# Six parameter loads issued by ScalarE's queue instead of SP's at the start of a hybrid S5 / RG-LRU / PEER step

## The chip, the cores and the metric

One core of a Trainium2 chip runs the whole kernel; the other cores are idle. The metric is the device time of one execution in microseconds. The kernel before takes 3084.43 us, the median of three runs (3083.14 to 3085.8). Its engines are TensorE (PE), VectorE (DVE), ScalarE (ACT), GpSimd (POOL) and SyncE (SP), each with its own instruction stream, and 16 DMA engines that serve transfers issued by any of them.

## The reference, cut to what matters

One layer over 1024 prompt tokens and 8 decode tokens, all in float32, width 1024:

```python
def layer(x, ...):
    h = rmsnorm(x, norm_mix)
    proj = h @ w_in                       # 1024 x 3584
    u_s5, x_lru, y_lru, g_a, g_b = jnp.split(proj, SPLITS, axis=-1)
    a_out, s5_re, s5_im = s5_branch(u_s5, h0_re, h0_im, lam_re, lam_im, log_dt, ...)
    b_out, lru_h, new_buf = rglru_branch(x_lru, y_lru, conv_buf, lru_h0, ...)
    merged = (jax.nn.sigmoid(g_a) * (a_out @ w_proj_a)
              + jax.nn.sigmoid(g_b) * (b_out @ w_proj_b))
    x = x + merged @ w_out
    x = x + peer(rmsnorm(x, norm_ffn), w_q, sub_keys, u_tab, v_tab)   # 8 heads x 16 experts a token
    return x, (s5_re, s5_im, lru_h, new_buf)
```

The parameters that matter here are small: `log_dt` (one value per S5 group), `lam_re` and `lam_im` (the S5 eigenvalues), `norm_mix` (the gain of the first norm), and a packed table of biases and convolution weights. The S5 branch needs `exp(lam * exp(log_dt))` before it can scan; the first projection needs `x * norm_mix`.

## The kernel before, in words

The prompt is worked in chunks of 256 tokens (four of them, the last with the 8 decode tokens beside it). A chunk runs the norm, the projections, the S5 and RG-LRU branches, the mixing, the PEER queries and the choice of experts; then its 256 gather slots (one indirect transfer each, 128 rows of 8 KB) are used by DVE (dot products) and PE (weighted sums), interleaved with the dense work of the next chunk. The first chunk's dense work has no gathers beside it.

What matters here is the first 20 us. Each engine's stream is written out by hand.

SP (from line 620) first issues the two halves of the first chunk's columns of x, 512 KB each, as 128 rows of 4 KB (line 622). Then come the six small parameter loads (lines 645 to 648): two halves of `log_dt`, each one 64-byte row broadcast to 64 partitions, then `lam_re`, `lam_im`, `prm` and `nmix`, each 128 short rows. All six count on one semaphore, `step_in`. Then the loop over `load_weights(0, l)` issues the first two pairs of weight blocks of `w_in`, 1024 KB each as 128 rows of 8 KB (line 634). Then eight more parameter loads (line 653) and one for the block-diagonal gate weights (line 654). Later weight loads wait until PE has freed a slot of the ring (`slot_free`).

ACT's stream starts at line 1176: a dummy square root of one column, which makes the first table load happen early; then the squares of the two halves of x (`norm_squares`), each as soon as its half has landed; then it waits for `step_in`, and makes eight blocks of `raw`, that is x times `nmix`, at 0.41 us a block; then the square root of the norm (`norm_root`). All its activations have line 807 in the profile.

DVE's stream starts at line 1253 with two memsets, then waits for `step_in` (all six loads) before anything else: the exponential of `log_dt` by a polynomial, `norm_mean` (which needs PE's sum of squares), more small parameter work, the reciprocal of the norm (line 1246), and `first_units(0)` (line 1212), which needs PE's first projected unit.

PE's stream: warm-up matmuls on ones (line 2457 on), the sum of squares (`norm_sum`, line 2012), and then the units of the first projection (line 2037). A unit's matmul t waits for block t of `raw` and, at its start, for its weights.

Of the kernel before, what the change touches and what calls it, by code (L numbers as in the profile page):

```python
# [356 lines left out]
def build(nc, i_, o_):  # L357

    with ExitStack() as ctx:
# [6 lines left out]
        def sem(name):  # L366
            return ctx.enter_context(nc.semaphore(name))
# [47 lines left out]
        nmix = T.take(KT)  # L415
        nffnT, nfinT = T.take(KT), T.take(KT)
        prm = T.take(40)
# [20 lines left out]
        lre, lim, ldt, th = (S.take(SJ) for _ in range(4))  # L438
# [73 lines left out]
        step_in = sem("step_in")  # L512
# [83 lines left out]
        def flat(v):  # L596
            return v.rearrange("p a b -> p (a b)")
# [21 lines left out]
        def _(sp):  # L619
# [22 lines left out]
                    before = c if at >= 0 else c - 1  # L642
                    sp.wait_ge(unit, units(before) + slot_unit(before, PAIRS[before][at][-1]) + 1)

            for g2 in range(2):
                sp.dma_start(ldt[64 * g2:64 * g2 + 64, :], i_["log_dt"][g2].partition_broadcast(64)).then_inc(step_in, 16)
            for name, dst in (("lam_re", lre), ("lam_im", lim), ("prm", prm), ("nmix", nmix)):
                sp.dma_start(dst, i_[name]).then_inc(step_in, 16)
            for l in range(2 * RING):
                load_weights(0, l)  # L650
            for name, dst in (("b_raw", braw), ("c_raw", craw), ("s5_0", s0), ("sconv", sconv), ("slru", slru),
# [153 lines left out]
        def _(act):  # L805
# [215 lines left out]
            def chunk(c, last):  # L1021
# [149 lines left out]
                if last:  # L1171

                    act.wait_ge(s8_out, 16 * HEADS)
                    act.dma_start(flat(sS[0:NS * HEADS, 0:2]), s8_dram.rearrange("t h k -> (t h) k")).then_inc(s8_in, 16)

            act.sem_inc(sum_ok, 1)
            act.wait_ge(const_ok, 1)
            af(rt2, ones[:, 0:1], ACT.Sqrt)
# [1372 lines left out]
```

## Time and profile before

| | |
|---|---|
| median of three runs | 3084.43 us (3083.14 to 3085.8) |
| span of the profiled execution | 3084.7 us |
| PE busy, matmuls | 2367.6 us, 77% |
| DVE busy | 2150.7 us, 70% |
| POOL busy | 1202.5 us, 39% |
| ACT busy | 1001.2 us, 32% |
| DMA | 1226.32 MB, mean 398 GB/s |
| DMA queue of POOL (q0) | 148608 packets, 1082.20 MB |
| DMA queue of SP (q1) | 27440 packets, 136.67 MB |
| DMA queue of ACT (q10) | 1648 packets, 4.85 MB |

The page gives no time for the profiled execution other than its span, 3084.7 us, which lies 0.3 us above the median and inside the three runs. Busy time is the time in which an engine worked; the chain of waits is the path of work and releases that ended last, followed back from the end. The shares are of the whole span, and the change touches less than its first hundredth, so the page as a whole says little; the rows below are of the stretches that count.

### The profile page before, as it was taken

The page shows a single profiled execution, that of the slowest core. Times are in us where ns is not written, and L with a number is a line of the kernel's source. Part 1 is how long each engine was busy: PE and PEld are TensorE (multiplying, and loading weights), DVE is VectorE, ACT ScalarE, POOL GpSimd, SP SyncE. Part 2 cuts the span into 40 slices and gives each one's busy share as a digit, 9 for nine tenths or more (in the row PEclk, how much of TensorE's full clock was granted, in tenths as well). Part 3 has the DMA queues.
Part 4 walks back from the last instruction along what each step waited for, and adds up shares of the span by engine and source line. Part 5 has one row for each costly group of instructions (what it writes and reads, how often), then busy time and mean ns, then how long its engine had stood idle before and what let it go on. Part 6 is the DMA issues. An engine that isn't in the chain of part 4 may idle for free.

```text
span 3084.7 us, 40759 instructions
## 1 busy us (share of the span) xinstructions
PE 2367.6 (77%) x14560; PEld 1190.1 (39%) x14560; DVE 2150.7 (70%) x5361; ACT 1001.2 (32%) x3275; POOL 1202.5 (39%) x1048
## 2 busy tenths in 40 slices
PE   9997769888876778789777678888987676555565
PEld 7864325555343334455233324444433331111111
DVE  7758887765579887665468887766558897544445
ACT  2224332422334332432234332432233443222223
POOL 0013343443344443343343443434344444444442
PEclk9999889999999989989988879999998886777777
DMA  4569999999999999999999999999999999999997
GB/s 154 208 244 398 420 421 420 415 414 399 420 420 418 420 420 419 418 392 420 420 419 417 421 420 408 420 394 420 418 420 420 420 416 419 416 406 420 420 419 328
DMA packets 177898, 1226.32 MB, mean 398 GB/s; under 512 B 22664, under 2 KB 23048, under 8 KB 32160
## 3 DMA queue, kind: packets, MB, share of 16 engines
q0 software_dynamic: 148608, 1082.20, 84.9%
q1 hardware_dynamic: 27440, 136.67, 11.2%
q10 hardware_dynamic: 1648, 4.85, 0.4%
q8 instruction: 115, 1.88, 0.3%
q14 instruction: 87, 0.71, 0.1%
HBM read 1219.09 MB, written 4.55 MB: 397 GB/s over the span
## 4 chain that ended last, share of the span: by engine, by line
DMA 45%; PE 26%; DVE 15%; ACT 5%; POOL 3%; issue 3%; ACTq 1%; DVEq 0%; SPq 0%; POOLq 0%
DMA arena<-in_uv,arena 44%; PE psum L2140 11%; DVE arena L1718 7%; PE psum L2037 7%; ACT arena L807 4%; POOL arena L759 3%; PE psum L2184 3%; DVE arena L1212 3%; PE psum L2204 2%; DVE arena L1220 1%; DMA arena<-in_w_ab 1%; PE psum L2216 1%; ACT L807 1%; ACTq L831 1%; DVE arena L1590 1%
## 5 line engine op out<-in xcount | busy, mean ns | idle before, releaser
L759 POOL DMA_INDIRECT arena<-in_uv,arena x1032 | 1199.3, 1162 | 1856.2 <-PE psum L2140 1525.3
L1718 DVE CUSTOM_DVE_ANT_0 arena<-arena 128x1024 f32<-128x1024 f32 x1024 | 1246.8, 1225 | 789.4 <-DMA arena<-in_uv,arena 781.5
L2140 PE MATMUL psum<-arena 64*64 64x512 f32 x8184 | 1226.7, 723 | 669.9 <-ACT arena L807 622.5
L807 ACT ACTIVATE arena<-arena 128x1 f32<-128x1 f32 (+4 forms) x2746 | 727.1, 302 | 1850.8 <-DVE arena L1718 1741.9
L2140 PEld LDWEIGHTS psum<-arena 64*64 64x64 f32 x8184 | 301.2, 151 | 1401.1 <-ACT arena L807 923.5
L2037 PE MATMUL psum<-arena 128*128 128x256 f32 (+1 forms) x2656 | 632.4, 393 | 7.7 <-ACT arena L807 6.9
L2037 PEld LDWEIGHTS psum<-arena 128*128 128x128 f32 x2656 | 504.3, 194 | 193.6 <-issue 121.8
L1212 DVE TENSOR_TENSOR arena<-arena 128x256 f32<-128x256 f32 (+12 forms) x561 | 249.9, 472 | 12.1 <-issue 0.4
L807 ACT ACT_TABLE_LOAD x119 | 152.7, 1283 | 11.2 <-DVE arena L1212 7.1
L807 ACT ACTIVATE arena<-psum 128x256 f32<-128x256 f32 (+5 forms) x254 | 98.3, 402 | 144.9 <-PE psum L2037 94.4
L2184 PE MATMUL psum<-arena 128*128 128x128 f32 (+2 forms) x640 | 123.6, 351 | 9.5 <-DMA arena<-in_w_ab 7.2
L2184 PEld LDWEIGHTS psum<-arena 128*128 128x128 f32 x640 | 103.2, 196 | 37.2 <-issue 19.4
L1220 DVE SCALAR_TENSOR_TENSOR arena<-arena 128x256 f32<-128x256 f32 (+8 forms) x287 | 99.0, 357 | 19.3 <-ACT arena L807 13.9
L2204 PE MATMUL psum<-arena 128*128 128x512 f32 x192 | 90.3, 614 | 0.0
L1718 DVE DVE_READ_ACCUMULATOR2_ANT arena<- 128x1 f32 x1024 | 83.6, 82 | 0.0
L1486 DVE TENSOR_TENSOR_SCAN arena<-arena 128x64 f32<-128x64 f32 x256 | 68.9, 331 | 1.3
L1220 DVE SCALAR_TENSOR_TENSOR arena<-arena,psum 128x128 f32<-128x128 f32 (+4 forms) x97 | 46.0, 513 | 33.6 <-PE psum L2184 28.9
L2216 PE MATMUL psum<-arena 128*128 128x256 f32 (+1 forms) x320 | 63.2, 354 | 0.4 <-issue 0.4
L1212 DVE TENSOR_TENSOR arena<-psum,arena 128x512 f32<-128x512 f32 (+2 forms) x91 | 59.6, 684 | 2.8 <-PE psum L2140 1.8
L2216 PEld LDWEIGHTS psum<-arena 128*128 128x128 f32 x320 | 52.6, 200 | 22.5 <-issue 17.8
L2204 PEld LDWEIGHTS psum<-arena 128*128 128x128 f32 x192 | 35.2, 193 | 56.3 <-issue 56.3
L2052 PEld LDWEIGHTS psum<-arena 32*128 32x128 f32 x512 | 35.0, 207 | 28.9 <-issue 26.2
(134 smaller groups left out, 981.9 us busy)
## 6 DMA issues: line engine op xcount, KB each, us to landing
arena<-in_w_in SPq DMA_DIRECT2D x56, 1024.0 KB, 9.0
arena<-in_w_q SPq DMA_DIRECT2D x34, 1024.0 KB, 9.4
arena<-in_uv,arena POOLq DMA_INDIRECT x1032, 13.7
arena<-in_w_ab SPq DMA_DIRECT2D x12, 1024.0 KB, 9.4
arena<-in_w_out SPq DMA_DIRECT2D x11, 512.0 KB, 15.8
arena<-in_keys SPq DMA_DIRECT2D x17, 256.0 KB, 8.3
arena<-in_w_ab SPq DMA_DIRECT2D x8, 512.0 KB, 10.8
arena<-in_x_tok SPq DMA_DIRECT2D x8, 512.0 KB
```

What stands on the lines that cost most here:

```text
L759: pool.indirect_dma_start(uvring[:, r], None, i_["uv"], bass.IndirectOffsetOnAxis(column, 0)).then_inc(uv_in[r], 16)
L807: return nc.scalar.activation(out, in_, f, **kw)
L1212: return V.tensor_tensor(out, a, b, op)
L1220: return V.scalar_tensor_tensor(out=out, in0=a, scalar=s1, in1=b, op0=op0, op1=op1)
L1486: return V.tensor_tensor_scan(v, mag2[:, j:j + 1].to_broadcast([P, SEG]), v, start, ALU.mult, ALU.add)
L1718: V.tensor_tensor_reduce(out=u, in0=u, in1=hn[i // (SLOT // 2)], scale=1.0, scalar=0.0, op0=ALU.mult, op1=ALU.add, accum_out=dots_[:, b % ...
L2037: ins = mm(PB[u % 2][:, 0:n], w[:, P * t:P * t + P], rhs[:, t, 0:n], start=(t == 0), stop=(t == k - 1))
L2052: ins = mm(SB[j % 2][:, 2 * SEG * part:2 * SEG * part + 2 * SEG], wT[o:o + 32, QT * (2 * r + part) + q], uS[o:o + 32, q, 2 * SEG * r:2 * S ...
L2140: ins = mm(PV[o:o + HP, half], dg[r:r + HP, PAIR * (b % 2) + k], uvring[r:r + HP, place(c, i) % UV, at:at + 512], start=(i % (SLOT // 2) = ...
L2184: ins = mm(banks[side][:, 0:cols.stop - cols.start], w[:, 512 * side + P * t:512 * side + P * t + P], src[:, t, cols], start=(t == 0), sto ...
L2204: ins = mm(OUTB[t][half][0:rn], hT[c][:, k, r0:r0 + rn], w[:, 512 * half:512 * half + 512], start=(k == 0), stop=(k == KT - 1))
L2216: ins = mm(PB[s][:, 0:n], w[:, P * t:P * t + P], gb[:, t, cols], start=(t == 0), stop=(t == KT - 1))
```

## The change

The six small loads leave SP's stream and are issued at the head of ACT's stream, ahead of its first activation, in the same order and on the same semaphore. SP's stream goes from the columns of x straight to the first two weight loads. Nothing else is different: who waits for `step_in`, and for how much of it, is the same.

```diff
@@ -642,10 +642,6 @@
                     sp.wait_ge(unit, units(before) + slot_unit(before, PAIRS[before][at][-1]) + 1)
 
-            for g2 in range(2):
-                sp.dma_start(ldt[64 * g2:64 * g2 + 64, :], i_["log_dt"][g2].partition_broadcast(64)).then_inc(step_in, 16)
-            for name, dst in (("lam_re", lre), ("lam_im", lim), ("prm", prm), ("nmix", nmix)):
-                sp.dma_start(dst, i_[name]).then_inc(step_in, 16)
             for l in range(2 * RING):
                 load_weights(0, l)
@@ -1173,6 +1169,10 @@
+            for g2 in range(2):
+                act.dma_start(ldt[64 * g2:64 * g2 + 64, :], i_["log_dt"][g2].partition_broadcast(64)).then_inc(step_in, 16)
+            for name, dst in (("lam_re", lre), ("lam_im", lim), ("prm", prm), ("nmix", nmix)):
+                act.dma_start(dst, i_[name]).then_inc(step_in, 16)
             act.sem_inc(sum_ok, 1)
             act.wait_ge(const_ok, 1)
             af(rt2, ones[:, 0:1], ACT.Sqrt)
```

## Rows read from the trace of the kernel before

**Rows 1.** Page, part 4: the chain that ended last, by engine.

```profile
DMA 45%; PE 26%; DVE 15%; ACT 5%; POOL 3%; issue 3%; ACTq 1%; DVEq 0%; SPq 0%; POOLq 0%
```

**Rows 2.** Busy time in three stretches: length, busy us of each engine, granted clock, DMA share, GB/s.

```profile
14.00:91.00 77.00, 74.61 (x636) 61.51 (x636) 68.25 (x207) 24.02 (x46) 0.00 (x0) 1.00 0.34 116
91.00:205.00 114.00, 110.61 (x793) 93.97 (x790) 70.52 (x239) 16.87 (x41) 7.93 (x8) 1.00 0.53 202
205.00:645.00 440.00, 353.85 (x2232) 185.14 (x2231) 349.44 (x940) 168.70 (x524) 174.30 (x154) 0.91 1.01 415
```

**Rows 3.** Who waited for whom from 14 to 91 us: us in total, times, longest.

```profile
PE psum L2052 <- DVE arena L1212: 1.1, 1, 1.1
...
DVE arena L1216 <- issue: 0.5, 1, 0.5
```

**Rows 4.** SP's issues in order of time: start us, us, what; idle before and its releaser.

```profile
0.75 0.89 SPq L622 DMA_DIRECT2D arena<-in_xT  x2
1.68 1.23 SPq L646 DMA_DIRECT2D arena<-in_log_dt  x2
...
4.53 0.43 SPq L648 DMA_DIRECT2D arena<-in_nmix  x1
5.00 0.91 SPq L634 DMA_DIRECT2D arena<-in_w_in  x2
```

**Rows 5.** ACT in order of time, from the start.

```profile
0.83 1.28 ACT L807 ACT_TABLE_LOAD   x1 [0.83 <-PEq L2533]
...
4.49 1.06 ACT L807 ACTIVATE arena<-arena 128x1024 f32<-128x1024 f32 x1 [2.16 <-DMA arena<-in_xT]
5.83 4.32 ACT L807 ACTIVATE arena<-arena 128x1024 f32<-128x1024 f32 x9 [0.29 <-DMA arena<-in_xT]
```

**Rows 6.** DVE in order of time, three of its groups up to 14.5 us.

```profile
6.86 0.42 DVE L1217 TENSOR_SCALAR arena<-arena 128x16 f32<-128x16 f32 x2 [5.94 <-DMA arena<-in_nmix]
...
10.12 0.42 DVE L1217 TENSOR_SCALAR arena<-psum 128x256 f32<-128x256 f32 x1
...
14.05 0.42 DVE L1212 TENSOR_TENSOR arena<-psum,arena 128x256 f32<-128x256 f32 x1
```

**Rows 7.** PE in order of time: sum of squares, then the first projection.

```profile
6.04 3.62 PE L2012 MATMUL psum<-arena 128*128 128x256 f32 x16
10.21 20.00 PE L2037 MATMUL psum<-arena 128*128 128x256 f32 x90 [0.56 <-DMA arena<-in_w_in]
```

**Rows 8.** DMA from 0 to 60 us: issues, KB each, median us to landing.

```profile
arena<-in_c_raw SPq DMA_DIRECT2D x1, 512.0 KB, 8.0
arena<-in_b_raw SPq DMA_DIRECT2D x1, 256.0 KB, 7.4
...
arena<-in_nmix SPq DMA_DIRECT2D x1, 4.0 KB, 2.3
```

**Rows 9.** DMA packets from 1.7 to 4.95 us, then from 4.95 to 6.05 us.

```profile
DMA packets 329, 1.02 MB, mean 314 GB/s; under 512 B 81, under 2 KB 81, under 8 KB 329
...
DMA packets 695, 0.08 MB, mean 72 GB/s; under 512 B 687, under 2 KB 687, under 8 KB 695
```

**Rows 10.** DMA queues from 2470.2 to 2480.7 us: packets, MB, share of 16 engines.

```profile
q0 software_dynamic: 595, 4.33, 97.7%
q1 hardware_dynamic: 597, 0.04, 3.9%
```

**Rows 11.** DMA queues from 2397 to 2398 us, the same columns.

```profile
q0 software_dynamic: 26, 0.20, 49.3%
q1 hardware_dynamic: 20, 0.14, 33.7%
q10 hardware_dynamic: 22, 0.09, 22.2%
```

**Rows 12.** DMA from 2567.5 to 2574 us: an issue of ACT, KB, us to landing.

```profile
arena<-s_scratch ACTq DMA_DIRECT2D x1, 64.0 KB, 6.2
```

**Rows 13.** DMA packets from 6.05 to 12 us.

```profile
DMA packets 308, 2.15 MB, mean 362 GB/s; under 512 B 25, under 2 KB 25, under 8 KB 52
```

## The prediction

> **What bounds the kernel now.** I read the chain of waits first, by engine [rows 1]: the gathers' transfers lead, then PE, then DVE. Then the busy time by stretch [rows 2]: the DMA engines are at a third of their time from 14 to 91 us, at half from 91 to 205, and full from 205 on. What to see: the long part is a stream of gathers with the DMA engines full, and it can begin only when the first chunk's dense work is done. It has no slack against the start, so whatever the start loses or gains is passed on to the end one for one. The share of DMA is low before 205 us because the ring of weights is refilled only as PE frees it, so the DMA engines can't work ahead during a delay.
>
> Then the waits from 14 to 91 us [rows 3]. DVE waits there for no other engine (its longest entry is 0.5 us of its own issue); PE waits once for DVE, 1.1 us. So from 14 to 91 us DVE sets the pace, and from 91 us PE does (110.61 of 114 us busy [rows 2]), released by DVE. The start of that chain is DVE's first projected unit at 14.05 us [rows 6]. Two paths meet there. One is DVE's own: it idles 5.94 us for the last small load, starts at 6.86, and reaches 14.05 after 7.19 us of its own instructions. The other is PE's: sum of squares from 6.04 to 9.66, 0.56 us of idle for the first weights, first unit from 10.21 [rows 7] with 16 matmuls at 0.233 us, 3.73 us, so ready at 13.94. They tie. The change can gain only if both get earlier.
>
> **The change, part by part.**
>
> SP: the six issues took from 1.68 to 5.00 us [rows 4], 3.32 us. Gone, they bring the first weight issue from 5.00 to 1.68, and those behind it forward by as much. The first weights then follow x in the DMA engines without the gap. That takes away PE's 0.56 us of waiting; by itself it gives nothing, since DVE's own path ties.
>
> ACT: six issues now stand ahead of the table load that ran from 0.83 [rows 5]. At SP's pace they take 3.3 us, to 4.1 us; bounds are nothing (if the table load stands first and hides most of them) and twice SP's time, since both queues issue at once here and no row shows that. Load 1.28 and dummy root 0.2 follow, so the squares of the first half begin at 5.6 instead of 4.49, and of the second at 6.6 instead of 5.83. PE's sum of squares, which began 0.5 us after its first half was squared, moves from 6.04 to 6.7 and ends at 10.3; `norm_mean` on DVE from 10.12 to about 10.4. That costs 0.3 us if nothing else is later, and the PE start stays at 10.2. This term is covered by the next one.
>
> The small loads themselves, the term that decides. Before, they stood in SP's queue behind x and ahead of the weights: after x's last packets at 4.95 us they ran alone, and were through by 5.9 [rows 9]. Counted in packets, the rows under 512 B are 81 and 687, 768 in all: 640 rows of parameters, and the completions of the six and of x's two halves. That is 46 small packets to each of 16 engines (40 rows and 6 completions). `nmix`, issued at 4.53, was landed at 6.86, 2.3 us later [rows 8], some 0.9 us behind its last packet. After the change they are in ACT's queue, and SP's queue has x, the weights, `b_raw` and `c_raw` behind each other with no gap. How do the engines share between two queues? By the packet, not by the byte: from 2470.2 to 2480.7 us SP's queue carries small outputs beside the gathers, and the counts are 597 against 595, though the small ones are 0.04 MB and the large 4.33 MB [rows 10]. Each small packet waited for one large one. With the two hardware queues and the gathers together the counts of a microsecond are 20, 22 and 26 [rows 11], so ACT's queue and SP's take turns too. And a transfer of ACT of 64 KB, 5 packets an engine, took 6.2 us to land when the engines were full [rows 12], against the 2.3 us of `nmix`.
>
> So 46 small packets an engine must alternate with SP's large ones, first 4 KB of x, then 8 KB of weights. From x, 18 turns an engine are to be had (8 rows and a completion for each half), but the small ones are issued from 0.8 to 3.7 us and reach the engines at least 1 us later, while x runs from 1.8 to 5; I take 12 small ones served when x ends (bounds 18, if every turn is used, and 7, if they begin as late behind a full queue as in rows 12). That leaves 34: 18 go with the two weight loads (16 rows and 2 completions an engine), 9 with `b_raw`, 7 with `c_raw`. In time: x ends at 4.95 plus 12 small packets at 0.02 (687 of them took 0.95 us over 16 engines, so 0.02 each), 5.2. Weights 2.1 MB at 400 GB/s, 5.25 us, to 10.45. `b_raw` 256 KB, 0.66 us, to 11.1. Seven rows of 4 KB of `c_raw`, 0.16 us each, 1.15 us, to 12.25. The 34 small packets between them 0.7 us, to 12.95; landing 0.9 us, 13.8. Bounds: with 18 served early, 28 are left, 18 + 9 + 1, which ends at 12.0 and lands at 12.9; with 7 served early, 39 are left, and they last through `c_raw` and three rows of the next load, 14.2, or 14.8 at the 362 GB/s at which the weights came before [rows 13]. I take 13.7.
>
> The Trainium skill, page "DMA: Bandwidth & Descriptors", section "Queues, rings and completion order", says that an engine goes round its queues by whole packets, typically 9 to 17 descriptors, before it changes. The counts above can't tell single rows from such bundles. By that rule each small transfer would take one turn, behind x's halves, the two weight loads, `b_raw` and `c_raw` in turn, and the last would land at about 14.0 us: the same side, 0.3 us later. The same page, section "Issuing engines are not separate DMA queues", warns that issuing from several engines saves only issue time.
>
> What waits for `step_in`: all of it, so for the last. On DVE the whole stream stands behind it (exponential, mean, reciprocal, first unit, and everything after). On ACT the eight blocks of `raw` and the root stand behind it, and PE's first unit behind the first block. With `step_in` at 13.7 us: `raw` 13.7 to 17.0, PE's first unit 14.15 to 17.9, `norm_mean` at 13.7 + 3.26 = 17.0, root at 17.4, first unit on DVE at 13.7 + 7.19 = 20.9 instead of 14.05. DVE's own path is the longer by 3 us, so it sets the shift: 13.7 - 6.86 = 6.8 us. PE moves by only 3.9 us, and waits longer for DVE where it waited 1.1 us [rows 3]; it can't make the rest good. The weights, now landed by about 9 us, have nobody who could use them yet.
>
> **Sum.** The profiled execution: 3084.7 + 6.8 = 3091.5. The median is 0.3 us lower: 3091.2. Bounds of the term: step_in at 12.9 gives 3090.4, at 14.8 3092.3; twice SP's issue time on ACT would put the last small issue at 6.6 and its packets at 7.6, still before the engines' backlog ends, and adds at most 1 us.
>
> A measurement of this kernel tells about 0.2% from no change, 6.2 us; the forecast, 0.22%, lies right at it.
>
> **The rivals.**
>
> (a) The small packets slip in without waiting. Then `step_in` comes at about 6 us (3.7 + 2.3), only ACT's late squares count, and the time is 3084.4 + 0.3 = 3084.7, no change. For it: in rows 10 and 12 the other queue was POOL's with rows of 8 KB, and at the start the first rows are of 4 KB. Against it: rows 11, where ACT's and SP's queues take turns as well.
>
> (b) The other side: faster. The same free passage, and the table load stands ahead of the six issues and runs beside them. Squares are then as early as before, PE starts at 9.5 and DVE at 6.5: the first unit at 13.7, 0.4 us earlier, 3084.0. It decides only if `step_in` is landed before 6.86. Against it: the issues are written ahead of the activation that needs the table. No path here is worth more than 0.6 us of gain, since the sum of squares at 9.66 holds both.
>
> (c) The delay is there but PE's shift, not DVE's, reaches the end, because DVE has room that the profile doesn't show: 3.9 us, 3088.3. For it: PE is busy 74.61 of 77 us. Against it: DVE waits for nobody [rows 3].
>
> (d) More than forecast: the issues of both queues slow each other, or the table load comes first and holds the issues by 1.3 us. Then 3092 to 3094.
>
> **How the numbers follow.** Forecast, turn by turn, 0.66, its own range 3090.2 to 3092.5; (a) 0.12; (b) 0.06; (c) 0.09; (d) 0.07. The predicted time is the forecast's, 3091.2. The range for 8 in 10 takes in (c) and most of (a), and some of (d): 3084.3 to 3093.5. The bound of 0.2% is 3090.6; the forecast lies above it with three quarters of its weight, 0.48, and (d) adds 0.05: slower 0.53. The rest of the forecast, (a), (c) and nearly all of (b) are no measurable change: 0.44. Faster by over 0.2% has no term here, 0.03 for what I don't see.
>
> **What the profile would show.** SP's first weight issue at 1.7 us. Six issues of ACT from 0.8 to about 4.1, the table load behind them, the first squares at 5.6. DVE's first TENSOR_SCALAR at 13.7 (12.9 to 14.8), after an idle of some 12.7 us put down to `nmix`; PE idle from 10.3 to 14.1, put down to ACT; DVE's first unit at 20.9; PE's wait for DVE grown from 1.1 to some 4. In the queues, between 5 and 10 us, as many packets of ACT's queue as of SP's. The forecast is wrong if DVE starts before 8 us, or if it starts at 13 and the stretch from 205 us on has not moved by as much.

## The result and the profile after

The changed kernel takes 3093.82 us, median of nine runs (3091.39 to 3094.95); the kernel before, run beside it, 3085.46 us (nine runs). The ratio is 1.0027, 95% interval 1.0018 to 1.0036: 8.4 us slower (5.6 to 11.1), and 0.3 us beyond the upper end of the stated range. The profiled execution's span is 3092.1 us, 7.4 us over the one before. A span is 2.2 to 2.6 us shorter than the device time of the same execution (here 3092.1 against 3094.44), so the 3084.7 of before belongs to an execution of about 3087.1, an estimate, and not to one at the median. Each trace is of one execution, and its distance from the median of its kernel has to be kept in mind below.

The start in order of time: start us, us, engine, line, operation, idle before and its releaser. It answers to [rows 4 to 7].

```profile
0.75 0.88 SPq L622 DMA_DIRECT2D arena<-in_xT  x2
0.76 1.20 ACTq L1173 DMA_DIRECT2D arena<-in_log_dt  x2
...
1.68 1.02 SPq L634 DMA_DIRECT2D arena<-in_w_in  x2
...
3.76 0.74 ACTq L1175 DMA_DIRECT2D arena<-in_nmix  x1
...
4.62 1.28 ACT L803 ACT_TABLE_LOAD   x1 [4.62 <-issue]
...
7.11 3.72 PE L2012 MATMUL psum<-arena 128*128 128x256 f32 x16 [0.60 <-ACT arena L803]
...
14.79 0.43 DVE L1217 TENSOR_SCALAR arena<-arena 128x16 f32<-128x16 f32 x2 [13.87 <-DMA arena<-in_nmix]
...
15.44 9.84 PE L2037 MATMUL psum<-arena 128*128 128x256 f32 x34 [4.61 <-ACT arena L803]
...
21.91 0.42 DVE L1212 TENSOR_TENSOR arena<-psum,arena 128x256 f32<-128x256 f32 x1
```

SP's first weight issue is at 1.68 us as meant. But `nmix`, issued at 3.76, a little earlier than before (4.53), lands 11.0 us later instead of 2.3. DVE idles 13.87 us for it, and its first unit is at 21.91 instead of 14.05 us: 7.9 us late.

The DMA queues from 8 to 11 us: packets, MB, share of 16 engines.

```profile
q1 hardware_dynamic: 167, 1.24, 97.5%
q10 hardware_dynamic: 169, 0.01, 3.8%
```

SP's queue (q1) and ACT's (q10) take turns: as many packets of the one as of the other, mostly 8 KB rows on SP's side and rows of 32 to 160 bytes on ACT's. That a turn is a single row is shown at e6 below. The delay is then passed on whole. The first gather, in the kernel before and in the changed one:

```profile
188.67 1.09 POOL L759 DMA_INDIRECT arena<-in_uv,arena  x1 [184.82 <-DVEq L1655]
```

```profile
196.50 1.09 POOL L755 DMA_INDIRECT arena<-in_uv,arena  x1 [192.65 <-DVEq L1655]
```

That is 7.8 us later, and the end 7.4.

### The profile page after: what moved, and what is told of

Its sections match the earlier page's. It is cut to its first block, busy times and chain, and to the rows that moved or that the text cites. A ratio compares the mean times of both kernels' runs of the same rounds, so it can differ in the third digit from the quotient of the medians.

```text
span 3092.1 us, 40759 instructions
## 1 busy us (share of the span) xinstructions
PE 2362.6 (76%) x14560; PEld 1186.1 (38%) x14560; DVE 2151.0 (70%) x5361; ACT 1000.9 (32%) x3275; POOL 1206.4 (39%) x1048
## 3 DMA queue, kind: packets, MB, share of 16 engines
q1 hardware_dynamic: 26704, 136.62, 11.1%
## 4 chain that ended last, share of the span: by engine, by line
DMA 46%; PE 26%; DVE 15%; ACT 4%; POOL 4%; issue 3%; ACTq 1%; DVEq 0%; POOLq 0%
DMA arena<-in_uv,arena 44%; PE psum L2140 11%; DVE arena L1718 7%; PE psum L2037 7%; POOL arena L755 4%; ACT arena L803 4%; PE psum L2184 3%; DVE arena L1212 3%; PE psum L2204 2%; DVE arena L1220 1%; DMA arena<-in_w_ab 1%; PE psum L2216 1%; DVE arena L1590 1%; PE psum L2076 1%; ACTq L827 1%
## 5 line engine op out<-in xcount | busy, mean ns | idle before, releaser
L803 ACT ACT_TABLE_LOAD x119 | 152.7, 1283 | 14.8 <-DVE arena L1212 7.0
L803 ACT ACTIVATE arena<-psum,arena 128x256 f32<-128x256 f32 (+2 forms) x64 | 27.2, 448 | 56.1 <-PE psum L2223 29.1
```

What stands on the lines that cost most here:

```text
L803: return nc.scalar.activation(out, in_, f, **kw)
```

## The experiments

Three things were to be told apart: the turns between two queues; ACT's issuing as such; and a pause that the forecast had not: from 5 to 6 us the changed kernel's DMA engines are half idle (a share of 0.47), although x, the first weights and all six small loads have been issued. The three columns of times in the table are DVE's start, which is the last small load's landing, DVE's first unit, and the first gather.

| run | landed | first unit | first gather | time (median), ratio and interval |
|---|---|---|---|---|
| before | 6.86 | 14.05 | 188.67 | |
| changed | 14.79 | 21.91 | 196.50 | 3093.82, 1.0027 (1.0018 to 1.0036) |
| e1 weights wait | 6.95 | 15.64 | 190.30 | 3087.15, 1.0006 (0.9997 to 1.0015) |
| e2 weights first, one queue | 13.19 | 20.33 | 194.96 | 3092.85, 1.0022 (1.0013 to 1.0031) |
| e3 two packed loads on ACT | 6.21 | 14.06 | 188.71 | 3083.82, 0.9997 (0.9987 to 1.0006) |
| e4 two packed loads on SP | 6.14 | 13.67 | 188.32 | 3084.93, 0.9995 (0.9986 to 1.0004) |
| e5 SP's other loads wait | 13.00 | 20.13 | 194.74 | 3090.79, 1.002 (1.001 to 1.003) |
| e6 plain log_dt | 12.19 | 19.32 | 193.91 | 3091.6, 1.0021 (1.0012 to 1.0031) |
| e7 27 packets | 6.35 | 14.15 | 188.75 | 3088.15, 1.001 (1.0001 to 1.002) |
| e8 log_dt on SP | 7.62 | 14.75 | 189.35 | 3085.72, 1.0003 (0.9993 to 1.0012) |
| e9 log_dt last | 12.98 | 20.09 | 194.66 | 3093.62, one run |
| e10 only log_dt on ACT | 7.35 | 14.48 | 189.05 | 3085.83, one run |
| e11 plain log_dt on SP | 9.86 | 16.99 | 191.56 | 3084.62, one run |

The kernel before took 3085.5 beside e1 to e4, 3084.64 beside e5 to e8, 3085.28 beside the last three. The first three columns are of one execution each; its device time lies within 1.6 us of the median, except in e7, where it lies 3.5 us below.

**e1: the weights wait for the small loads.**

```diff
+            sp.wait_ge(step_in, 16 * 6)
             for l in range(2 * RING):
                 load_weights(0, l)
```

> The changed kernel, but SP waits for all six small loads before it issues the first weights, so ACT's small transfers share the DMA engines with x alone. Turn-taking theory: the small loads are landed at about 6.5 us (not 14.8), the weights are issued then and land 5.2 us later, PE's first projected unit starts at about 12 and is used by DVE at 15.8 (14.05 before, 21.91 changed): 3087 us, some 6 us under the changed kernel. Rival (ACT's issues are slow or its queue is slow by itself): the small loads land after 10 us, and the time is 3092 or more.

Landed at 6.95 with the same six issues on ACT, and the first unit at 15.64, as expected. The queues from 5 to 6 us, while the last of x goes through:

```profile
q10 hardware_dynamic: 650, 0.04, 44.3%
q1 hardware_dynamic: 41, 0.11, 27.6%
```

650 small packets in a microsecond, where the changed kernel served 43. So ACT's issuing is not what holds them; what stands in the other queue is.

**e2: one queue, the small loads behind the weights.** On SP, the loop over `load_weights` and the six loads change places.

> The kernel before, with the same six loads in SP's own queue but behind the first two weight loads instead of ahead of them: first in, first out, no second queue. Theory: the last small load lands right behind the second weight load, at about 12.2 us; DVE's first unit at 12.2 + 7.2 = 19.4; 3085.5 + 5.3 = 3090.8 us. The weights should follow x with no pause in the DMA engines. Rival (a pause between x and the weights comes with the weights' own early issue, whoever issues the small loads): there is the same pause of 1 to 1.5 us from 5 to 6.5 us as in the changed kernel, and the last small load lands at 13.5 or later.

Landed at 13.19, a microsecond later than expected; no pause behind x. SP's queue from 5 to 6 us:

```profile
q1 hardware_dynamic: 63, 0.42, 100.5%
```

So the weights' early issue makes no pause between x and the weights. With one queue the early weights delay the landing by 6.3 us just as well: what is needed first must not stand behind, or beside, 2 MB that nobody waits for yet.

**e3 and e4: two packed transfers.**

```diff
+        tpack = T.take(3 * KT + 40)   # nmix, nffnT, nfinT, prm
+        spack = S.take(3 * SJ)        # lre, lim, ldt (log_dt expanded)
...
+            for name, dst in (("spack", spack), ("tpack", tpack)):
+                act.dma_start(dst, i_[name]).then_inc(step_in, 16)
```

e4 has the same with `sp`, between x and the weights. In both, `nffnT` and `nfinT` ride in `tpack`, so SP has seven further parameter loads instead of nine.

> The changed kernel with the small loads packed by layout into two transfers of 128 rows (lam_re, lam_im and log_dt in one; nmix, the two other norm gains and prm in the other), issued by ACT. 18 small packets an engine instead of 46. Turn-taking theory: they are through with the last of x and the first 6 rows of the weights, landed at 7 to 8.3 us, DVE's first unit at 14.2 to 15.5, 3085.6 to 3087. Rival (bytes or the issuing queue count, not packets): landed at 13 or later, time as the changed kernel, 3093.

> The kernel before with the same two packed transfers in SP's queue, between x and the weights. Landed at about 6.1 us, the weights issued at 2.7 instead of 5.0; PE's first unit starts at 9.5 to 9.7, DVE's first unit at 13.7 instead of 14.05, limited by the sum of squares: 3085.1 us, 0.4 under the kernel before, which is not to be told from no change by time. Rival (the start has more to give): over 2 us faster.

Both carry more bytes than the six loads and both are landed earlier than before; e3, at 6.21, is even below the 7 to 8.3 expected. e3 has ACT's queue beside x and the weights, as the changed kernel has, with 18 small packets an engine instead of 46, all of them through by 6 us. e4's first unit is at 13.67, as expected. Neither is told from the kernel before by time; both are faster than the changed kernel.

**e5: SP's nine further loads wait for step_in.**

```diff
+            sp.wait_ge(step_in, 16 * 6)
             for name, dst in (("b_raw", braw), ("c_raw", craw), ("s5_0", s0), ("sconv", sconv), ("slru", slru),
```

> The changed kernel, but SP issues its nine further parameter loads only after the six small loads have landed; x and the two weight loads stay beside them. Turn-taking theory: up to the end of the weights at about 11 us it goes as in the changed kernel (22 small packets an engine served), then the remaining 24 are alone and through in 0.5 us: landed at 12.4, not 14.8; DVE's first unit at 19.6; 3085.5 + 5.5 = 3091 us, 2.4 under the changed kernel. Rival (nine issues of SP at the same time slow ACT's issues and the generation of descriptors, and that is what holds the small loads): the pause in the DMA engines from 5 to 6.5 us is gone, and they are landed by 11 us or before.

Landed at 13.00. ACT's queue from 11 to 12 us, where the weights end: the backlog leaves at once.

```profile
q1 hardware_dynamic: 31, 0.14, 33.6%
q10 hardware_dynamic: 327, 0.03, 22.7%
```

The pause is still there (DMA share 0.89, 0.63 and 0.72 in the microseconds from 4, 5 and 6 us on), so SP's further issues don't make it. Landing is 0.6 us later than expected.

**e6: log_dt as one plain load.** The host stores it expanded to 128 rows; one load replaces the two broadcasts, 45 packets an engine instead of 46. (The two waits for `step_in` ask for five loads, not six.)

```diff
-                act.dma_start(ldt[64 * g2:64 * g2 + 64, :], i_["log_dt"][g2].partition_broadcast(64)).then_inc(step_in, 16)
+            for name, dst in (("log_dt", ldt), ("lam_re", lre), ("lam_im", lim), ("prm", prm), ("nmix", nmix)):
```

> The changed kernel with log_dt stored expanded and loaded in one plain transfer of 128 rows, instead of two that read one row of 64 bytes 64 times: five transfers, 45 small packets an engine instead of 46. Theory of the second term: the pause of SP's queue between x and the weights, from 5 to 6.5 us, and the small number of packets of ACT's queue from 4 to 5 us (18) come from the two broadcasts. Then without them the turns begin at once as in the packed kernel, 18 an engine by 6 us, 15 more with the weights to 10.9, 12 with the next two loads to 12.3: landed at 13.2; DVE's first unit at 20.4, 3091.8 us. Rival (the pause comes from two queues issuing at once): landed at 14.5 to 15, 3093.

The stretches from 4 to 7 us, a microsecond each (length, PE, PEld, DVE, ACT, POOL busy, clock, DMA share, GB/s), of the changed kernel:

```profile
4.00:5.00 1.00, 1.00 (x3) 0.77 (x3) 0.00 (x0) 0.38 (x1) 0.00 (x0) 1.00 1.01 333
5.00:6.00 1.00, 1.00 (x4) 0.67 (x2) 0.00 (x0) 0.99 (x2) 0.00 (x0) 1.00 0.47 146
6.00:7.00 1.00, 0.52 (x2) 0.00 (x0) 0.00 (x0) 1.00 (x3) 0.00 (x0) 1.00 0.86 313
```

and of e6:

```profile
4.00:5.00 1.00, 1.00 (x4) 0.79 (x4) 0.00 (x0) 0.99 (x3) 0.00 (x0) 1.00 1.07 419
5.00:6.00 1.00, 0.72 (x5) 0.29 (x3) 0.00 (x0) 0.89 (x1) 0.00 (x0) 1.00 1.08 427
6.00:7.00 1.00, 1.00 (x5) 0.90 (x6) 0.00 (x0) 0.88 (x1) 0.00 (x0) 1.00 1.03 421
```

The pause is gone, and landing is at 12.19, 1.0 us before what was expected and 2.6 us before the changed kernel's. What is left, 12.19 against 6.86, is the turns alone. These are single executions, and e6's is 1.6 us below its median; by the medians, each against the kernel before beside it, the broadcasts cost 1.4 us (8.4 less 7.0, each uncertain by some 3 us). The queues of e6 from 8 to 11 us:

```profile
q1 hardware_dynamic: 270, 1.18, 95.4%
q10 hardware_dynamic: 270, 0.02, 6.4%
```

Equal counts over 3 us could also come of turns of several rows each. So look at stretches shorter than one large row, which takes 0.31 us here; from 8.4 to 8.6 us, and from 8.6 to 8.8:

```profile
q1 hardware_dynamic: 7, 0.06, 69.1%
q10 hardware_dynamic: 7, 0.00, 3.1%
...
q1 hardware_dynamic: 12, 0.10, 115.9%
q10 hardware_dynamic: 11, 0.00, 4.8%
```

In all 21 stretches of 0.2 us from 5.8 to 10 us the two counts differ by at most 2. If an engine let eight small rows through at once, at 14 ns each, and then eight large ones, the small ones would come in eights. A turn is one row.

**e7: 27 packets.** ACT issues `spack`, `prm` and `nmix`.

> A dose between: ACT issues three plain transfers of 128 rows (lam_re, lam_im and log_dt packed; prm; nmix), 27 small packets an engine. Turn-taking theory: 18 served by 6 us, the other 9 take a turn each behind 8 KB of weights, 0.33 us, to 9.0: landed at 9.9 us; DVE's first unit at 17.1; 3085.5 + 3.0 = 3088.5 us. Rival (not counted by packets): as the two packed transfers, landed at 6.5 and 3084 to 3085.5, or as the six, 14.8.

In the trace the expected landing, 9.9, was missed: 6.35. The queues from 1 to 2 us:

```profile
q1 hardware_dynamic: 4, 0.02, 16.6%
q10 hardware_dynamic: 51, 0.01, 8.3%
```

ACT's queue got in ahead of x here, while e6's had no packet before 2 us. It had 110 through by 3 us where e6 had 21, and finished its 27 an engine by 6 us, with the first of the weights. Turns with x are nearly free, and only those left when the 8 KB rows begin cost a third of a microsecond. But this execution, at 3084.63 us, is the fastest of ten; the median is 3088.15, against the 3088.5 that was expected with a landing at 9.9. So the trace refutes the landing for one execution only. That ACT's early start is missing in the others would account for their 3.5 us over the kernel before; no trace shows it, and it stays open.

**e8 and e11: log_dt on SP, four plain loads on ACT.** In e8 the broadcasts stand in SP's queue between x and the weights; in e11 one plain load does.

> The changed kernel with the two broadcasts of log_dt left in SP's queue between x and the weights; ACT issues the other four (36 small packets an engine). If the broadcasts make the pause only in ACT's queue: 18 by 6 us, 15 with the weights to 10.9, 3 more: landed at 12.1 us, first unit 19.3, 3090.8 us. If the pause comes from the two queues issuing at once: still there from 5 to 6.5 us, landed at 13 to 14.

> Four plain loads on ACT as in the run with log_dt on SP, and log_dt as one plain load of 128 rows in SP's queue between x and the weights. If the broadcasts made the pause of that run (DMA 45% busy from 5 to 7 us): it is gone, all is landed at 6.3 to 6.8, weights by 9.5, first unit at 13.8 to 14.1. If the two queues make it: it stays and the last load lands after 7.5.

The expectations were wrong in both, and in a telling way. In e8 ACT's queue has an early start as in e7, 48 packets by 2 us; then the broadcasts make SP's queue pause, and ACT's small packets use the pause: all but 7 of its 576 are through by 7 us, and log_dt is the last to land, at 7.6. In e11 there is neither, the weights come at once, and `nmix` takes turns with them: landed at 9.86. From 7 to 8 us of e11:

```profile
q1 hardware_dynamic: 43, 0.35, 100.6%
q10 hardware_dynamic: 43, 0.00, 2.4%
```

With e7 and e6 this is a series of plain loads: 27, 36 and 45 packets an engine on ACT land at 6.35, 9.86 and 12.19, the first of them with its early start.

**e9 and e10: the broadcasts last, and alone.** e9 issues the four plain loads first; e10 leaves them on SP and gives ACT only the two broadcasts.

> The changed kernel with ACT's order turned: the four plain loads first, the two broadcasts of log_dt last. If the broadcasts make the pause: none in SP's queue from 4 to 6 us, small and large packets one for one from the start, and the last load (a broadcast) lands at 12.2 to 14 us. If any first transfer of ACT's queue makes it: the pause stays at 5 to 6.5 us and landing is at 14.8.

> Only the two broadcasts go to ACT's queue (10 small packets an engine), the four plain loads stay in SP's queue between x and the weights. If a broadcast beside another queue makes the pause: SP's queue under half busy somewhere from 4 to 6.5 us, log_dt landed at about 8, first unit at 15.3. If it takes the number of turns: landed at 6.5 to 7, first unit at 14.05.

In e9 the pause moves to where the broadcasts are served, and landing, 12.98, is in the range expected. (Its one time, 3093.62, is no lower than the changed kernel's median, though it lands 1.8 us earlier; a single execution can't tell that.) Of e9, the same columns as above:

```profile
5.00:6.00 1.00, 1.00 (x4) 0.67 (x2) 0.00 (x0) 0.99 (x3) 0.00 (x0) 1.00 1.09 438
...
10.00:11.00 1.00, 0.43 (x2) 0.02 (x1) 0.00 (x0) 0.00 (x0) 0.00 (x0) 1.00 0.71 197
11.00:12.00 1.00, 0.00 (x0) 0.00 (x0) 0.00 (x0) 0.00 (x0) 0.00 (x0) 1.00 0.52 157
```

In e10, 10 packets an engine on ACT are enough for it, but it costs less than expected: log_dt was to land at about 8, and it was `nmix`, on SP, that landed last, at 7.35; the first unit was at 14.48 and not at 15.3. Of e10:

```profile
4.00:5.00 1.00, 1.00 (x4) 0.79 (x4) 0.00 (x0) 0.49 (x1) 0.00 (x0) 1.00 0.85 325
5.00:6.00 1.00, 1.00 (x6) 0.62 (x5) 0.00 (x0) 0.57 (x1) 0.00 (x0) 1.00 0.69 159
```

So the pause goes with the broadcasts. They also get fewer turns beside x: with them at the head of ACT's queue it passes 18 to 32 packets from 4 to 5 us (the changed kernel, e1, e5, e10), with a plain load 87 (e6). A second busy queue is not what the slow stretch needs: e2 has one queue, and its microsecond from 10 us, where the small loads stand behind the weights, has a DMA share of 40%. Nor are the broadcasts always slow in one queue. The kernel before, from 5 to 5.2 us:

```profile
q1 hardware_dynamic: 222, 0.03, 96.3%
```

There, and in e1, the first weights were not issued until 5.00 and 6.94 us; in all runs with a slow stretch their issue had begun by 3.7 us, before most of the broadcasts were served. Whether that is the condition, and why the engines then fall idle, no run shows. The small packets themselves are not longer in the pause: 43 take 2.4% of the engines' microsecond, 9 ns each.

## Why the prediction was wrong in size and right in kind

The place and the mechanism held: `step_in` is what decides; the small packets take turns with SP's; DVE's whole stream stands behind them and its delay reaches the end. Point by point.

SP: the first weights at 1.68 us, worth nothing, as forecast. ACT: six issues from 0.76 to 4.50 instead of to 4.1, some longer than SP's were (0.74 for `nmix`, against 0.43 [rows 4]; in e1, without the weights' issues beside them, the six end at 4.03), the table load behind them, PE's sum of squares at 7.11 instead of the 6.7 forecast. Covered by the next term, as said.

The step that failed is the size of the term that decides, the landing of the small loads: 13.7 us forecast (its own working adds up to 13.8), bounds 12.9 to 14.8; measured 14.79. Two errors partly cancel, as far as single traces tell. The turns alone, without the broadcasts, land at 12.19 (e6), 1.5 us earlier than worked out and below the lower bound: by 5 us ACT's queue had 220 packets through, 14 an engine, and not 12 at 5.2. And the two broadcasts, which the prediction counted like any other 4 rows an engine, so that they had no price of their own, cost 2.6 us more (14.79 against 12.19; 1.4 by the medians). No row of before warned of it: in [rows 9] they went through without a pause.

From landing to the end: 14.79 - 6.86 = 7.9 us, first unit 7.86 later, first gather 7.83, span 7.4, median 8.4. The shift is passed on one for one, as forecast, within what the time can tell. In e2, e5 and e6 the first gather is 6.3, 6.1 and 5.2 us later and the time 7.4, 6.2 and 7.0, which is the same within 1.8 us. The forecast was 3091.2 and the median is 3093.82: 1.1 of the 2.6 us are the landing; 1.0 is the kernel before, 3084.43 in the three runs that it was worked out on and 3085.46 in nine; 0.5 is not accounted for. Without either of the first two the median would lie inside the range, which ended at 3093.5. That it lies just outside and not just inside is chance, since 0.3 us is far less than the interval leaves open.

One step was wrong without effect on the sum: PE was to be 3 us ahead of DVE, and to wait some 4 us for it later. Its wait there is still 1.07 us, because the room is used up earlier. In e6, at full clock, PE begins 2.6 us later than in the kernel before and DVE 5.3, and PE waits 2.21 us for ACT at 33.09 us. In the changed kernel the clock took most of the room, as the last section shows, and that wait is 0.47 us.

The rivals: (a) and (b), free passage, are refuted by the counts of packets, though e7's trace shows free passage for 27 packets that come early. (c), that PE's shift sets the end, can't be told by the changed kernel, where PE came to be 7.4 us late as well; e5 and e6 refute it: PE's first unit begins 3.4 and 2.6 us later, DVE's 6.1 and 5.3, the first gather 6.1 and 5.2. (d) named other reasons for its 3092 to 3094; ACT's issues did end 0.4 us later than forecast, which decided nothing, since `step_in` came later still.

The Trainium skill, page "DMA: Bandwidth & Descriptors", section "Queues, rings and completion order", has engines change queue at whole packets, typically 9 to 17 descriptors. By that rule ACT's queue should deliver a load's eight rows an engine in one turn. The trace doesn't agree: in e6 the counts of the two queues are 7 and 7, then 12 and 11, in stretches of 0.2 us, shorter than one large row, so the turns here are single rows. The counts of 3 us alone, 270 and 270, would be as good for bundles.

## What to carry to other kernels

A second queue doesn't bring many small rows past large ones. In these runs the DMA engines share by packets, so a load of many short rows beside one of long rows pays one long row for each short one: count packets, not bytes, before splitting queues. Pack small parameters into few rows, expand a small broadcast on the host when it shares the start with large loads, and keep in front of everybody only what the first waiter needs; a large load issued early is a cost to each small one beside or behind it. And before a trace is read against a median, see where the traced execution lies among the others: e7's was 3.5 us below.

## What the runs showed that was not expected

The granted clock fell. In 4.61 us of idle, from 10.83 us on, it went from 1.00 to 0.50 at 13.2 us; PE's first projected unit began at 15.44 us at 0.50, which is 1.2 of 2.4 GHz, and it stayed there until 20 us. The changed kernel:

```profile
16.00:18.00 2.00, 2.00 (x6) 1.64 (x5) 1.40 (x8) 2.00 (x6) 0.00 (x0) 0.50 0.00 0
18.00:20.00 2.00, 2.00 (x6) 1.55 (x6) 1.50 (x8) 0.50 (x2) 0.00 (x0) 0.50 0.00 0
20.00:22.00 2.00, 2.00 (x11) 1.77 (x10) 1.89 (x3) 0.00 (x0) 0.00 (x0) 0.99 0.00 0
```

Six matmuls in 2 us against 11 at full clock, each time with those cut by the ends. PE had done 20 by 22.26, 6.82 us for what takes 4.6 at full clock: 2.2 us, so that it was 7.4 us behind its old time instead of 5.2. It cost nothing here, because DVE was later still, 7.9 us; with a path of DVE's shorter by more than 0.5 us it would have, by this working. e2 and e9 show the same fall, to 0.50 in the two microseconds from 14 to 16, after PE had idled 3.49 and 3.20 us; in e5 and e6, where it had idled 3.0 and 3.18 us, the clock stayed at 1.00.
